# The first and the last mixer of a twelve-stage transformer kernel: weight blocks split one by one between the steps of two heads

## The reference, cut to what matters

```python
def mixer_ab(h, qk_g, sink, conv_w, conv_b, rel_table):        # first mixer
    q, k, v = split_qkv(h, qk_g)
    att = windowed_attention(q, k, v, sink, rel_table)          # 8 query heads, 2 key heads
    gb, gc, u = jnp.split(h[..., QKV_COLS:], 3, axis=-1)
    conv = gb * short_conv(gc * u, conv_w, conv_b)
    return jnp.concatenate([att, conv], axis=-1)

# one head of attention, in both: s = q.k * scale + bias, masked
    p = jnp.exp(s - mx)
    den = jnp.sum(p, axis=-1, keepdims=True) + jnp.exp(sk - mx)
    o = jnp.einsum('bnhgqk,bnkhd->bnqhgd', (p / den).astype(v.dtype), vb)

def swa_sink_mixer(u, table, w_in, sinks, w_out):               # last mixer
    q, k, v = jnp.split(u @ w_in, _offsets(ODD_SIZES), axis=-1)
    ...
    o, lse = banded_attention(q, k, v, bias, C_WINDOW - 1)
    o = o * jax.nn.sigmoid(lse - sinks.astype(F32))[..., None]
    return o.reshape(bn, S, C_HEADS * HEAD_DIM).astype(u.dtype) @ w_out
```

## Time and profile before

| What | us |
|---|---|
| median of three runs | 2114.94 |
| the profiled execution's own time | 2119.04 |
| its span in the trace | 2117.3 |
| TensorE busy (90% of the span) | 1912.7 |
| VectorE busy (68%) | 1436.4 |
| ScalarE busy (47%) | 989.7 |
| mean granted clock of TensorE | 0.949 of full speed |

### The profile page before, as it was taken

One profiled execution on the slowest core, in us unless ns is written; L12 is line 12 of the kernel. 1 busy time (PEld: TensorE's weight loads), 2 busy tenths in 40 slices (PEclk: granted clock), 3 DMA queues, 4 the chain that ended last, 5 costly groups with the idle time before them and its releaser, 6 DMA issues.

```text
span 2117.3 us, 38192 instructions
## 1 busy us (share of the span) xinstructions
PE 1912.7 (90%) x16458; PEld 1634.7 (77%) x16458; DVE 1436.4 (68%) x2248; ACT 989.7 (47%) x1591; POOL 6.5 (0%) x14
## 2 busy tenths in 40 slices
PE   3999878999999984799999998779999999969998
PEld 2888667888788862478888887547888888858887
DVE  6889675878798845566576666554766766765664
ACT  3444644445544540344455454324544545464543
POOL 0000000000000000000000000000000000000000
PEclk7999989999999996899999999779999999989999
DMA  8989432776699540336656554203555555432552
GB/s 322 390 339 362 175 149 98 291 281 239 241 366 360 224 182 0 120 143 226 234 181 223 195 193 179 91 30 120 196 195 207 182 207 209 152 118 91 217 200 80
DMA packets 54276, 423.98 MB, mean 200 GB/s; under 512 B 5955, under 2 KB 6131, under 8 KB 26683
## 3 DMA queue, kind: packets, MB, share of 16 engines
q1 hardware_dynamic: 52172, 413.59, 51.9%
q0 software_dynamic: 1936, 7.95, 1.0%
HBM read 420.38 MB, written 1.13 MB: 199 GB/s over the span
## 4 chain that ended last, share of the span: by engine, by line
PE 70%; DVE 16%; ACT 6%; DMA 5%; issue 2%; SPq 0%; DVEq 0%; ACTq 0%
PE pw L392 14%; PE pw L393 14%; PE pw L394 14%; PE acc L392 7%; PE acc L394 7%; PE acc L393 7%; DVE ring_lo L1349 6%; DMA land<-stream 4%; ACT ring_hi L1001 2%; DMA modw<-wmod 1%; PE acc L617 1%; DVE modw L1244 1%; PE pw L582 1%; PE pssq L460 1%; PE pw L585 1%
## 5 line engine op out<-in xcount | busy, mean ns | idle before, releaser
L392 PE MATMUL pw<-h_hi,ring_hi 128*128 128x256 bf16 x3248 | 892.8, 275 | 55.0 <-DVE h_lo L1335 36.5
L393 PE MATMUL pw<-h_lo,ring_hi 128*128 128x256 bf16 x3248 | 892.7, 275 | 0.0
L394 PE MATMUL pw<-h_hi,ring_lo 128*128 128x256 bf16 x3248 | 892.5, 275 | 0.0
L1349 DVE TENSOR_TENSOR ring_lo<-land,ring_hi 128x1024 bf16<-128x1024 f32 x633 | 737.6, 1220 | 191.9 <-ACT ring_hi L1001 191.4
L1001 ACT ACTIVATE ring_hi<-land 128x1024 bf16<-128x1024 f32 x633 | 622.1, 1045 | 234.6 <-DMA land<-stream 120.8
L392 PEld LDWEIGHTS pw<-h_hi,ring_hi 128*128 128x128 bf16 x3248 | 318.5, 98 | 118.8 <-issue 53.1
L392 PE MATMUL acc<-a_hi,ring_hi 128*128 128x256 bf16 x1408 | 384.9, 273 | 4.4 <-DVE a_lo L1399 4.4
L394 PE MATMUL acc<-a_hi,ring_lo 128*128 128x256 bf16 x1408 | 384.8, 273 | 0.0
L393 PE MATMUL acc<-a_lo,ring_hi 128*128 128x256 bf16 x1408 | 384.8, 273 | 0.0
L394 PEld LDWEIGHTS pw<-h_hi,ring_lo 128*128 128x128 bf16 x3248 | 319.7, 98 | 39.8
L393 PEld LDWEIGHTS pw<-h_lo,ring_hi 128*128 128x128 bf16 x3248 | 318.9, 98 | 38.5 <-issue 0.3
(11 more groups left out here) (230 smaller groups left out, 1557.7 us busy)
## 6 DMA issues: line engine op xcount, KB each, us to landing
land<-stream SPq DMA_DIRECT2D x211, 1536.0 KB, 6.5
modw<-wmod SPq DMA_DIRECT2D x144, 512.0 KB, 7.6
biasT<-bias_rows POOLq DMA_DIRECT2D x3, 1536.0 KB, 9.1
biasT<-bias_rows POOLq DMA_DIRECT2D x1, 3072.0 KB, 13.2
cst_s<-cst SPq DMA_DIRECT2D x1, 1792.0 KB, 10.1
x<-xT SPq DMA_DIRECT2D x1, 1024.0 KB, 9.7
out<-proj SPq DMA_DIRECT2D x1, 1024.0 KB, 3.9
par_s<-par SPq DMA_DIRECT2D x1, 699.0 KB, 13.8
```

Source lines behind the costliest of these rows:

```text
L392: mm(o, lhs[0], rhs[0], start=start, stop=False, skip_group_check=True)
L393: mm(o, lhs[0], rhs[1], start=False, stop=False, skip_group_check=True)
L394: return mm(o, lhs[1], rhs[0], start=False, stop=stop, skip_group_check=True)
L1349: v.tensor_tensor(ring_lo[:, t % RING, b, :], land[:, t % LAND, b, :], ring_hi[:, t % RING, b, :], ALU.subtract).then_inc(lo_ready, 1)
```

## The change

In both mixers the order of ScalarE's and VectorE's steps is rewritten. No instruction is added or removed, and the instructions of TensorE and SyncE keep their order. Splits that were done three blocks at a time are given to the steps as one or two blocks. In ab, the bias of pair 0 stands before the first convolution, and the denominators of a pair stand before the splits and the bias of the next pair; ScalarE does the exponentials first, then takes out the projection, splits, and copies. In sw, ScalarE splits a third whole triple before the first pair and then one block for each of the six pairs; VectorE's splits are put between the first evacuations, and in the loop behind the bias of a pair instead of ahead of it.

```diff
--- before.py
+++ after.py
@@ -1050,6 +1050,7 @@
                 t = FIRST[i] + 2
                 split_high(t)
                 split_high(t + 1)
+                split_high(t + 2)
                 for p in range(11):
                     if p >= 3:
                         pair_out(i, "sw", p - 3)
@@ -1057,8 +1058,8 @@
                         pair_exp(i, "sw", p)
                     if 1 <= p <= 8:
                         pair_copy(i, "sw", p - 1)
-                    if p in (1, 3, 5):
-                        split_high(t + 2 + p // 2)
+                    if p < 6:
+                        split_high(t + 3 + p // 3, blocks=(p % 3,))
                 split_high(t + 5)
 
             def mixer_ab(i):
@@ -1075,22 +1076,35 @@
                         split_high(t + n // 3)
                     evac(n)
                 inverse_root(sqh[:, 0:5, :], accv[:, 0:5, :], 1.0 / HD, 1)
-                for n in range(7, 11):
+                evac(7)
+                for n in range(8, 11):
                     evac(n)
-                    if n == 9:
-                        split_high(t + 3)
-                for p in range(7):
-                    if p < 4:
-                        for n in range(11 + 2 * p, min(13 + 2 * p, 18)):
-                            evac(n)
-                    if p >= 3:
-                        pair_out(i, "ab", p - 3)
-                    if p < 4:
-                        pair_exp(i, "ab", p)
-                    if 1 <= p <= 4:
-                        pair_copy(i, "ab", p - 1)
-                    if p < 3:
-                        split_high(t + 4 + p)
+                    split_high(t + 3, blocks=(n - 8,))
+                pair_exp(i, "ab", 0)
+                evac(11)
+                evac(12)
+                split_high(t + 4, blocks=(0,))
+                pair_exp(i, "ab", 1)
+                evac(13)
+                evac(14)
+                split_high(t + 4, blocks=(1, 2))
+                pair_copy(i, "ab", 0)
+                pair_exp(i, "ab", 2)
+                evac(15)
+                evac(16)
+                split_high(t + 5, blocks=(0,))
+                pair_out(i, "ab", 0)
+                pair_copy(i, "ab", 1)
+                pair_exp(i, "ab", 3)
+                evac(17)
+                split_high(t + 5, blocks=(1, 2))
+                pair_out(i, "ab", 1)
+                pair_copy(i, "ab", 2)
+                split_high(t + 6, blocks=(0,))
+                pair_out(i, "ab", 2)
+                pair_copy(i, "ab", 3)
+                split_high(t + 6, blocks=(1, 2))
+                pair_out(i, "ab", 3)
                 split_high(t + 7)
                 split_high(t + 8)
 
@@ -1611,24 +1625,25 @@
                     ins.then_inc(proj_evac, 1)
 
                 evac(0)
-                evac(2)
-                split_low(t)
-                evac(3)
-                evac(4)
-                evac(5)
+                split_low(t, blocks=(0,))
+                for n in range(2, 6):
+                    evac(n)
+                    split_low(t + (n - 1) // 3, blocks=((n - 1) % 3,))
                 dve.wait_ge(rsT_mm, 2)
                 v.tensor_copy(rsT[:], pssq[:, 0:TT]).then_inc(rsT_ready, 1)
                 dve.wait_ge(rsT_ready, 2)
                 evac(1)
+                split_low(t + 1, blocks=(2,))
+                later = [(t + 2, (0, 1)), (t + 2, (2,)), (t + 3, (0, 1)), (t + 3, (2,)), (t + 4, (0,)), (t + 4, (1,)), (t + 4, (2,))]
                 for p in range(11):
                     if 1 <= p <= 8:
                         pair_normal(i, "sw", p - 1)
                     if p < 4:
                         evac(6 + p)
-                    if p in (0, 2, 4, 6):
-                        split_low(t + 1 + p // 2)
                     if p < 8:
                         pair_bias(i, "sw", p)
+                    if p < 7:
+                        split_low(later[p][0], blocks=later[p][1])
                     if p >= 3:
                         pair_out(i, "sw", p - 3)
                 split_low(t + 5)
@@ -1651,18 +1666,29 @@
                 split_low(t)
                 head_norms(i, "ab", 1).then_inc(qk_ready, 1)
                 split_low(t + 2)
+                pair_bias(i, "ab", 0)
                 gate_conv(i, 0)
-                split_low(t + 3)
-                for p in range(7):
-                    if 1 <= p <= 4:
-                        pair_normal(i, "ab", p - 1)
-                    if p < 4:
-                        pair_bias(i, "ab", p)
-                    if p < 3:
-                        split_low(t + 4 + p)
-                        gate_conv(i, 1 + p)
-                    if p >= 3:
-                        pair_out(i, "ab", p - 3)
+                pair_normal(i, "ab", 0)
+                split_low(t + 3, blocks=(0, 1))
+                pair_bias(i, "ab", 1)
+                split_low(t + 3, blocks=(2,))
+                gate_conv(i, 1)
+                pair_normal(i, "ab", 1)
+                split_low(t + 4, blocks=(0,))
+                pair_bias(i, "ab", 2)
+                split_low(t + 4, blocks=(1, 2))
+                pair_normal(i, "ab", 2)
+                pair_out(i, "ab", 0)
+                gate_conv(i, 2)
+                pair_bias(i, "ab", 3)
+                split_low(t + 5, blocks=(0, 1))
+                pair_normal(i, "ab", 3)
+                pair_out(i, "ab", 1)
+                split_low(t + 5, blocks=(2,))
+                gate_conv(i, 3)
+                pair_out(i, "ab", 2)
+                split_low(t + 6)
+                pair_out(i, "ab", 3)
                 split_low(t + 7)
                 split_low(t + 8)
```

## The result

The changed kernel takes 2092.74 us (median of 4, 2090.26 to 2095.51) against 2115.64 (4 runs, 2112.21 to 2116.51): ratio 0.9892, 95% interval 0.9879 to 0.9905, 22.9 us less. Forecast were 2090.9 and 24.0 less. The profiled execution took 2092.54 us.

The account below looks back on a forecast made before the run. No engine is full in the two mixers; a chain of TensorE waits and the low clock behind them bounds them. 13.1 us (ab) + 10.9 (sw) = 24.0 off the median 2114.94 gives 2090.9 us, range 2084 to 2100.

Parts of the forecast that it names:

- The two stretches: ab from the chunk behind the head norms, sw from its seventh chunk, to the output projection: 13.1 and 10.9 us less.
- the seventh chunk: sw, TensorE: starts 2.8 us later, at the low clock after a 4.3 us wait, as rsT is copied later.
- bias 3: ab, VectorE: the bias of pair 3, done behind convolution 2, forecast to end at 298.4.
- The wait in front of values 2: ab, TensorE: 5.7 us, the largest wait left, with values 2 and turn 3 behind it at the low clock.
- hidden by 0.4 us: sw, ScalarE: the third triple's blocks end at 1853.8, before exponentials 0 can start, needing bias 0 at 1854.2.
- A: Rival: only ab gains, 13.1 us, time 2101.8 us; 5 in 100.
- B: Rival: only sw gains, 10.9 us, time 2104.0 us, as ab's wait of 5.7 us comes twice; 3 in 100.
- E: Rival: no change, the feed-forward behind each mixer takes the gain back by waiting for its weights; 2 in 100.
- D: Rival: short waits keep the granted clock at 0.50 through both mixers, 35 us slower, 2150 us; 2 in 100.
- C: Rival: ScalarE's blocks in ab cost less waiting, both mixers near upper bounds, 16 + 12.5: 2086.4 us; 4 in 100.
- 3 us either way: The other ten stages: allowance for where low-clock stretches lie once they start earlier, about two steps' worth.

Follow-up runs that it names:

- e1: Kernel before, with only mixer_ab of ScalarE and VectorE in the new order, mixer_sw as before; 2101.14 us, ratio 0.9937 to before.
- e2: Kernel before, with only mixer_sw of ScalarE and VectorE in the new order, mixer_ab as before; 2102.68 us, ratio 0.9941 to before.
- e4: Changed kernel, but in sw VectorE's copy of the transposed norm stands ahead of the second triple's three blocks; 2095.45 us, sw 3.9 us longer.
- e8: Changed kernel, but in sw ScalarE does exponentials 0 ahead of the third triple's split; 2097.91 us, sw 7.6 us longer.
- e11: Changed kernel, in sw transposed-norm copy and exponentials 0 moved ahead of splits, denominators 0 ahead of VectorE's third-triple blocks; 2096.74 us, sw 0.2 us longer.
- e5: Changed kernel, but in ab ScalarE does output 1 and copy 2 ahead of two blocks of the fourth triple; 2089.37 us, ab 107.47 for 107.46.
- e6: Changed kernel, but in ab VectorE does bias 3 ahead of convolution 2; 2084.21 us, ab 103.63 us, 3.8 us less.
- e9: Both mixers in a new searched order of the same instructions, against the kernel before; 2074.72 us, ratio 0.9805.

## Why the prediction was right

- **The two stretches**: 53.8 and 49.8 us forecast, 53.80 and 49.81 measured; e1 and e2 show that each comes from its own half. Following both engines' orders forward with start-to-start prices was enough here. That it came out to 0.1 us is partly luck: the forecast put the low clock on values 2 and turn 3 in ab and on the seventh chunk in sw, and there it fell. The same way of counting missed the size of e4, e8 and e11 by 0.2 to 2.4 us beyond the expected range, because it fell elsewhere.
- **ab**: bias 3 was forecast to end at 298.4 on the clock of before; it ended at 293.01, and 5.35 us are the shift of the stage (257.71 to 252.36), so 298.36. The wait in front of values 2 was 5.13 for 5.7, that in front of values 3 1.18 for 1.2, and none stood ahead. The prediction named two things late for the first wait, copy 2 behind the blocks and bias 3 behind the convolution. e5 and e6 show that the second decides.
- **sw**: the seventh chunk starts 2.6 us later in its stage (2.8 forecast), after 4.02 us of wait (4.3), at the low clock: 4.46 us for 2.79. Exponentials 0 were "hidden by 0.4 us" behind the third triple; ScalarE stood 0.75 us idle between the two. Biases 3 to 6 start at 1853.35, 1858.29, 1863.23 and 1868.16, 4.9 apart (5.0). By the Trainium skill's rule (TensorE: Matmul & The Clock Gate, section "HAM oscillation") the chunk behind the gap had to be slow, and the trace agrees for this gap of 4.02 us. Behind the seven waits of 0.96 to 2.52 us that follow, everything ran at the full clock. The prediction also said that this chunk at the full clock would be worth only 0.4 us in the sum, because exponentials 0 wait for the landed blocks. e4 bears that out in direction: its seventh chunk starts 2.3 us earlier and runs at the full clock (2.79 us), and turn 0 is only 0.9 us earlier.
- **Rivals**: A and B fall by e1 and e2, E by the stages behind the mixers (190.91 and 190.76 us behind ab, 169.30 behind sw in both), D by the granted clock of 0.94 and 0.97. C's size wasn't reached. Its mechanism, ScalarE's blocks costing less waiting than counted, isn't seen either: the largest wait of ab could be cut (e6), but by VectorE's order, and moving ScalarE's blocks gave nothing (e5). D's arithmetic was off: it took about 32 us for TensorE's work in sw at the full clock, and e9 shows 36.9 at a granted clock of 1.00; by D's own sums (78 us of work, 17 of waits, 130.4 us before) the change would turn into a loss below a mean clock of nearly 0.7, not 0.6.
- **The other stages**: 3 us either way were allowed. In the profiled pair they gave 2.4 of the span's 26.5: the first feed-forward gave 4.6, the time ahead of it 0.8, and the nine others took back 3.1, the most of them, 1.6, in the second mixer (stage 4), with 68.3 instead of 58.0 us of low clock. The medians differ by 22.9 where the mixers give 24.1. The prediction's reason, that each of the ten begins with a low stretch, was a wrong reading: in the trace of before stages 6, 8, 9 and 11 have none at all.

## What to carry to other kernels

Where no engine is full, write the two helper engines' orders down with start-to-start prices and follow them: it gave both stretches to 0.1 us when the low clock fell where it was put, and a search over such orders gave 13.8 us more in the two mixers. When a wait is named, look for what its releaser itself stood idle for, two or three links back: the copy got the name, the bias behind a convolution had the power. Edits that lose 3.9 and 7.6 us alone can lose almost nothing together with a third (e4, e8, e11), so undo an obstacle on all engines at once before judging it.

## What the runs showed of the hardware that was not expected

The low clock does not follow from the waits just ahead of it. In the same place of sw, with the same wait in front of values 6, 2.52 and 2.53 us, the changed kernel ran turn 7 in 1.61 us and e4 in 2.54; e11, with 2.53, in 2.93. A wait of 1.68 us in front of values 3 was followed by the low clock in e5 and not in the changed kernel, whose order in sw is the same. What differed was the history ahead of it. In e4 such stretches cost 4.8 us and in the changed kernel 1.7 (the seventh chunk), a difference of 3 us in one stage, as much as the orders under test; in e5 the extra one cost nothing. I found no rule in these traces that says beforehand where it falls.
